# Rotation angles and their sine moved behind the merge, between two modulation rows, in a transformer kernel on one Trainium2 core

## The chip, the cores and the metric

The kernel runs on one core of a Trainium2 chip, as one launch. The metric is the device time of that launch in microseconds (us), the median of several executions. The core has a matrix engine (TensorE, PE in the profile; its weight loads are listed apart as PEld), a vector engine (VectorE, DVE), an activation engine (ScalarE, ACT) and GpSimd (POOL). SyncE (SP) issues the transfers from device memory; each engine works through its own stream of instructions in order, and the streams meet at semaphores. TensorE's clock is granted at one of two levels, 1.2 or 2.4 GHz; the profile gives the granted clock as a share of the upper one.

## The reference

One block of a first kind and two layers of a second kind, on a sequence of 256 tokens and width 1024, in float32. The part around the change is the end of the first block's mixer and its output projection:

```python
merged = jax.nn.sigmoid(p_ga) * y_a + jax.nn.sigmoid(p_gb) * y_b   # y_a = (...) @ w_a, y_b = o @ w_b
x = x + gate_m[:, None, :] * rms_norm(merged @ w_out[i], g_post_mix[i])
h = modulate(rms_norm(x, g_pre_ffn[i]), shift_f, scale_f)
```

`shift_f`, `scale_f` and `gate_f` are parts of `mod = silu(c) @ w_ada + b_ada`. The two later layers turn their queries and keys with cosines and sines of `positions * inv_freq` (`cos, sin = rope_tables(positions)`). These tables depend on the inputs alone and are used for the first time in the first of the two later mixers, hundreds of microseconds after the place where they are made.

## The kernel before

Everything lies in `build`: one function per engine, with the stages as nested functions of the same names on each engine. The order of the work on an engine is the order in which its code is written; nothing schedules it. Waits are `wait_ge` on semaphores. A `v(...)` with `v.settle()` behind it makes VectorE's next instruction wait for the end of the last.

The stages around the change, in order:

- `rwkv` ends on VectorE with the group norm (L2160 to L2164: six times three operations of 128x256). On TensorE it ends with the gate tiles 9 to 15 (L878), which ScalarE takes out of PSUM with a sigmoid (L1509).
- `angles` (VectorE, L1785 to L1805) turns the positions into angles between minus pi and pi: one conversion, one multiplication and seven operations each for `sin2` and `cos2`, all 128x256, sixteen in all; then it signals `ang_ready`. Its scratch tiles and the positions lie in `arena`, apart from all that the merge uses.
- ScalarE loads the sine's table and computes the two sines in place (L1748, L1749), and signals `trig_ready`.
- `merge` computes sixteen products of 128x256 on TensorE (L1201), into the two PSUM banks 4 and 5 in turn. Product `n` waits until VectorE has read product `n - 2` (`ym_read`). Products 0 to 7 use `w_b` and the attention's output; products 8 to 15 use `w_a`, whose two halves are the ring slots of products 8 to 11 and 12 to 15. VectorE multiplies each product by its gate (L2171 for the first eight, L2175 for the rest) and GpSimd adds each of the last eight into `merged` (L2539).
- After each of the last eight products VectorE also computes one modulation row (`ada_late`, L1809: a dot product of a 128x1024 tile with the activated condition). Rows 27 to 31 follow the merge. The rows' weights come in four tiles; SyncE loads row `r` when row `r - 4` is done.
- The modulation of the FFN is made of rows 8 to 31 (L2375 to L2378), and signals `mod_ready`, for which TensorE waits in `hand_over` behind the projection.
- `project` (TensorE, L945) multiplies `merged` by `w_out` into banks 0 to 3, one after another. ScalarE, ahead of taking the squares of each bank (`rms_of_output`, L1518 to L1529), copies the first half of the FFN's first weights (`high_up`, L1422), and VectorE makes their remainder (`low_up`, L1841).

SyncE's queue (L647 for the ring of two weight slots, L697 for the modulation rows) issues in this order: `w_b` (freed by a gate tile), the first half of `w_a` (freed by the last gate tile), the second half of `w_a` (freed by product 7), rows 22 to 25, `w_out` (freed by product 11), rows 26 to 31, the first FFN weights (freed by product 15).

Of the kernel before, what the change touches and what calls it, by code (L numbers as in the profile page):

```python
# [246 lines left out]
G_FFN1 = G_GATES + 8  # L247
# [21 lines left out]
def wait(engine, sem, value):  # L269

    if isinstance(value, int) and value <= 0:
        return
    engine.wait_ge(sem, value)


def build(nc, T, out):
    with ExitStack() as ctx:
# [3 lines left out]
        def sem(name):  # L281
            return ctx.enter_context(nc.semaphore(name))
# [49 lines left out]
        def K(name, a=0, b=None):  # L332
            if name in EARLY_AT:
                at, w = EARLY_AT[name]
                return early[:, at + a:at + (w if b is None else b)]
            at, w = CONST_AT[name]
            return const[:, at + a:at + (w if b is None else b)]
# [139 lines left out]
        ym_full = sem("ym_full")  # L477
# [87 lines left out]
        def full_count(g, more=0):  # L565

            return 16 * (g // 2 + 1) + 8 * more
# [36 lines left out]
        def since(base, k):  # L604

            return base + max(k, 0)
# [803 lines left out]
        def _(act):  # L1410
# [6 lines left out]
            def high_up(f, g, c, h, i=0):  # L1417

                if h == 0:
                    act.wait_ge(slot_full[(g + c) % 2], full_count(g + c, i))  # L1420
                wait(act, half_done, 2 * FC * f + 2 * (c - 1) + h + 1 + 2 * i if c else 0)
                F(up_hi[:, h], ring[:, (g + c) % 2, h * 2048:(h + 1) * 2048], ACT.Copy).then_inc(up_high, 1)  # L1422
# [67 lines left out]
            def high_piece(j):  # L1490

                c, n = (j // 4, j % 4) if j < 36 else (9, j - 36)
                if n == 0 or j == 2:
                    act.wait_ge(slot_full[(G_MIX1 + c) % 2], full_count(G_MIX1 + c))
                if j > 34:
                    act.wait_ge(piece_used, j - 34)
                elif j > 4:
                    act.wait_ge(cm_full, j - 2)
                f(piece[j % 3][0], ring[:, (G_MIX1 + c) % 2, n * D:(n + 1) * D], ACT.Copy).then_inc(w_high, 1)

            def channel_major(table, base, qbase, part=range(64)):
                for j, (kind, q, _, dest) in enumerate(table):
                    if j not in part:
                        continue
                    act.wait_ge(cm_full, base + j + 1)
                    if q is not None:
                        wait(act, cm_out, since(qbase, q - 2))
                        dest = raw[:, q % 3, 1:S + 1]
                    f(dest, bank[4 + j % 2][:, 0:S], ACT.Sigmoid if kind == "sigmoid" else ACT.Copy).then_inc(cm_evac, 1)  # L1509
                    if table is T1 and j == KK_ROOT:  # L1510
                        act.wait_ge(kn_clamped, 1)
                        f(norm_kk, norm_kk, ACT.Sqrt).then_inc(kn_sqrt, 1)
                    if table is T1:
                        high_piece(j + 3)
# [229 lines left out]
            act.wait_ge(s_c, 48)  # L1744
            f(c_late, c_late, ACT.Silu).then_inc(c_ready, 1)
            channel_major(TG, CM_G, 0, range(9, 16))
            act.wait_ge(ang_ready, 1)
            f(sin2[:], sin2[:], ACT.Sin)  # L1748
            f(cos2[:], cos2[:], ACT.Sin).then_inc(trig_ready, 1)  # L1749
            act.wait_ge(ym_full, 16)  # L1750
            high_up(0, G_FFN1, 0, 0)
            rms_of_output(0, DONE_MIX1)
            norm(1, 1, 2, split_of=(0, G_FFN1))
            ffn_split(0, G_FFN1, G_LAYER)
# [17 lines left out]
        def _(dve):  # L1772
# [4 lines left out]
            def angles():  # L1777

                turn_hi = 6.28125
                turn_lo = 2 * math.pi - turn_hi  # L1780
                magic = 1.5 * 2.0 ** 23
                dve.wait_ge(s_lora, 32)
                dve.wait_ge(cm_evac, CM_G + 9)
                m = turns
                v(dve.tensor_copy(posf, pos_i))  # L1785
                v.settle()
                v(ts(ang, posf, K("inv_freq2"), None, ALU.mult))
                v.settle()
                for dst, quarter in ((sin2, 0.0), (cos2, 0.25)):
                    v(ts(m, ang, 1 / (2 * math.pi), quarter, ALU.mult, ALU.add))  # L1790
                    v.settle()
                    v(ts(m, m, magic, None, ALU.add))
                    v.settle()
                    v(ts(m, m, magic, None, ALU.subtract))
                    v.settle()
                    v(stt(posf, m, -turn_hi, ang, ALU.mult, ALU.add))
                    v.settle()
                    v(stt(posf, m, -turn_lo, posf, ALU.mult, ALU.add))
                    v.settle()
                    v(ts(posf, posf, quarter * 2 * math.pi, None, ALU.add))  # L1800
                    v.settle()
                    last = ts(dst[:], posf, math.pi, -math.pi, ALU.min, ALU.max)
                    v(last)
                    v.settle()
                dve.nop().then_inc(ang_ready, 1)  # L1805

            def dot(weights, c_of, out):

                return dve.tensor_tensor_reduce(out=weights, in0=weights, in1=c_of, scale=1.0, scalar=0.0, op0=ALU.mult, op1=ALU.add, accum_out=out)  # L1809
# [14 lines left out]
            def ada_late(r):  # L1824

                dve.wait_ge(apart_full[r % 4], 16 * (r // 4 + 1))
                dot(late_tile[r % 4], c_late, mod_raw[:, 0, 4 * FIRST + r:4 * FIRST + r + 1]).then_inc(apart_used, 1)
# [338 lines left out]
            def merge():  # L2166
                dve.wait_ge(cm_evac, CM_G + 16)
                for n in range(16):
                    dve.wait_ge(ym_full, n + 1)
                    if n < 8:  # L2170
                        tt(merged[:, n * S:(n + 1) * S], bank[4 + n % 2][:, 0:S], sig[:, (8 + n) * S:(9 + n) * S], ALU.mult).then_inc(ym_read, 1)  # L2171
                    else:
                        j = n - 8
                        wait(dve, ym_ready, j - 1)
                        tt(ytmp[:, n % 2], bank[4 + n % 2][:, 0:S], sig[:, j * S:(j + 1) * S], ALU.mult).then_inc(ym_read, 1)  # L2175
                        ada_late(19 + j)
# [190 lines left out]
            v(tt(mod_gate[:, 0], mod3[:, 0, 2], PR("g_post", 0, KD), ALU.mult))  # L2367
            attention1()
            rwkv()
            angles()  # L2370
            merge()
            for r in range(27, 32):
                ada_late(r)
            dve.wait_ge(apart_used, 4 * 8)
            v(tt(mod[:, 24:48], mod_raw[:, 0, 24:48], PR("b_ada1", 24, 48), ALU.add))  # L2375
# [203 lines left out]
```

## Time and profile before

| | us |
|---|---|
| median of 3 executions | 1742.59 |
| lowest, highest | 1742.31, 1746.23 |
| the profiled execution, its own time | 1739.06 |
| its span | 1737.3 |

The profile is one execution. Its page gives each engine's busy time as a share of the span, the granted clock, and the chain that ended last. Behind the page stand views of the trace: a timeline of instructions with the idle time before each and what ended it, a table by stretches of time, and the instructions of one line. All times are counted from the start of the span. The merge lies at about 366 to 403 us, the projection at 403 to 433.

### The profile page before, as it was taken

Reading aid. Unit: us, or ns where it says so; the run is one execution under the profiler, and the core shown is the slowest. Engines: PE = TensorE matmul, PEld = TensorE weight load, DVE = VectorE, ACT = ScalarE, POOL = GpSimd, SP = SyncE. Lnnn points to the kernel's source line nnn. Section 1 sums busy time; section 2 is a strip of 40 time slices with the busy share of each in tenths; the row PEclk is TensorE's granted clock in tenths of the full one; section 3 lists DMA queues with packets and bytes.
Section 4 is the critical chain, followed back from the end, with each engine's and each line's share of the span. In section 5 each row is a group of like instructions: output and inputs, shape, how many; then the busy total and the mean of one; then the engine's idle time right before and its main releaser. Section 6 shows DMA issues by size and latency. Waiting matters only on the chain.

```text
span 1737.3 us, 31528 instructions
## 1 busy us (share of the span) xinstructions
PE 1624.2 (93%) x12924; PEld 1438.9 (83%) x12924; DVE 1136.1 (65%) x1839; ACT 700.2 (40%) x1042; POOL 210.4 (12%) x273
## 2 busy tenths in 40 slices
PE   2998988889999989999998999999999999999998
PEld 2997777774899989999895599998999898579997
DVE  6796446374787877877565378778777665465454
ACT  2443433411533354333455443335333444543333
POOL 0342344222000000000115000000000002300000
PEclk9999999999999999999999999999999999999999
DMA  9754110256587837876440477774787542144531
GB/s 392 292 214 158 49 50 3 71 206 232 216 310 299 335 128 290 327 296 265 178 189 1 151 290 291 314 290 170 310 332 289 229 187 84 55 181 183 217 148 45
DMA packets 49638, 359.05 MB, mean 207 GB/s; under 512 B 5504, under 2 KB 6144, under 8 KB 29440
## 3 DMA queue, kind: packets, MB, share of 16 engines
q1 hardware_dynamic: 49536, 357.61, 53.5%
q8 instruction: 74, 1.21, 0.3%
q14 instruction: 28, 0.23, 0.0%
HBM read 356.54 MB, written 1.05 MB: 206 GB/s over the span
## 4 chain that ended last, share of the span: by engine, by line
PE 82%; DVE 8%; issue 4%; ACT 3%; DMA 1%; POOL 1%; SPq 0%; POOLq 0%; DVEq 0%; ACTq 0%
PE psum L840 11%; PE psum L842 11%; PE psum L841 11%; PE psum L853 5%; PE psum L854 5%; PE psum L855 5%; PE psum L945 5%; PE psum L878 3%; PE psum L810 2%; PE psum L1201 2%; DMA arena<-in_ada_head 1%; PE psum L1221 1%; PE psum L1222 1%; PE psum L1223 1%; PE psum L909 1%
## 5 line engine op out<-in xcount | busy, mean ns | idle before, releaser
L840 PE MATMUL psum<-split 128*128 128x256 f32 x1600 | 453.0, 283 | 2.8 <-DVE split L1841 2.8
L842 PE MATMUL psum<-split 128*128 128x256 f32 x1600 | 452.8, 283 | 0.0
L841 PE MATMUL psum<-split 128*128 128x256 f32 x1600 | 452.8, 283 | 0.0
L840 PEld LDWEIGHTS psum<-split 128*128 128x128 f32 x1600 | 307.0, 192 | 5.5 <-DVE split L1841 3.8
L1422 ACT ACTIVATE split<-ring 128x2048 fp32r<-128x2048 f32 x110 | 210.6, 1915 | 244.8 <-PE psum L842 169.2
L841 PEld LDWEIGHTS psum<-split 128*128 128x128 f32 x1600 | 307.0, 192 | 1.8
L842 PEld LDWEIGHTS psum<-split 128*128 128x128 f32 x1600 | 307.0, 192 | 0.0
L1841 DVE TENSOR_TENSOR split<-ring,split 128x2048 fp32r<-128x2048 f32 x110 | 251.8, 2289 | 76.4 <-ACT split L1422 73.2
L1861 DVE TENSOR_TENSOR split<-ring_down,split 128x2048 fp32r<-128x2048 f32 x55 | 126.0, 2292 | 116.9 <-ACT split L1430 116.9
L853 PE MATMUL psum<-split 128*128 128x512 f32 x440 | 171.8, 390 | 0.0
L854 PE MATMUL psum<-split 128*128 128x512 f32 x440 | 171.8, 390 | 0.0
L855 PE MATMUL psum<-split 128*128 128x512 f32 x440 | 171.2, 389 | 0.0
L1809 DVE CUSTOM_DVE_ANT_0 arena<-arena,c_row 128x1024 f32<-128x1024 f32 x144 | 167.6, 1220 | 0.0
L1430 ACT ACTIVATE split<-ring_down 128x2048 fp32r<-128x2048 f32 x55 | 105.3, 1915 | 136.5 <-PE psum L855 136.5
L2437 POOL TENSOR_TENSOR x_res<-x_res,scratch 128x512 f32<-128x512 f32 x16 | 20.4, 1274 | 1049.9 <-DVE scratch L1925 822.4
L1442 ACT ACTIVATE scratch<-psum 128x512 f32<-128x512 f32 x55 | 32.9, 599 | 213.1 <-PE psum L842 210.4
L855 PEld LDWEIGHTS psum<-split 128*128 128x128 f32 x440 | 82.6, 188 | 17.6
L853 PEld LDWEIGHTS psum<-split 128*128 128x128 f32 x440 | 82.8, 188 | 15.8
L854 PEld LDWEIGHTS psum<-split 128*128 128x128 f32 x440 | 82.8, 188 | 15.3
L878 PE MATMUL psum<-hT,ring 128*128 128x256 f32 x384 | 86.7, 384 | 3.0 <-ACT hT L1475 2.9
L878 PEld LDWEIGHTS psum<-hT,ring 128*128 128x128 f32 x384 | 73.2, 192 | 14.7 <-ACT hT L1475 3.2
L1850 DVE TENSOR_TENSOR scratch<-scratch,psum 128x512 f32<-128x512 f32 x55 | 37.8, 688 | 70.7 <-ACT scratch L1442 70.7
(422 smaller groups left out, 2897.6 us busy)
## 6 DMA issues: line engine op xcount, KB each, us to landing
ring<-in_up SPq DMA_DIRECT2D x55, 2048.0 KB, 10.4
arena<-in_ada SPq DMA_DIRECT2D x168, 512.0 KB, 6.4
ring_down<-in_down SPq DMA_DIRECT2D x55, 1024.0 KB, 4.9
ring<-in_in SPq DMA_DIRECT2D x19, 2048.0 KB, 7.9
ring<-in_gates SPq DMA_DIRECT2D x4, 2048.0 KB, 8.3
arena<-in_ada_head SPq DMA_DIRECT2D x4, 1536.0 KB, 16.8
ring_down<-in_w_out SPq DMA_DIRECT2D x3, 2048.0 KB, 12.0
ring<-in_w_out SPq DMA_DIRECT2D x3, 2048.0 KB, 8.7
```

What stands on the lines that cost most here:

```text
L840: mm(dst, up_hi[:, h, a], h_hi[:, kt_], start=(kt_ == 0 and j % 2 == 0), stop=False, skip_group_check=True)
L841: mm(dst, up_hi[:, h, a], h_lo[:, kt_], start=False, stop=False, skip_group_check=True)
L842: last = mm(dst, up_lo[:, h, a], h_hi[:, kt_], start=False, stop=(kt_ == KD - 1), skip_group_check=True)
L853: mm(bank[2 * t + h], act_hi[:, c % 2, a], d_hi[:, w], start=(c == 0 and k == 0), stop=False, skip_group_check=True)
L854: mm(bank[2 * t + h], act_hi[:, c % 2, a], d_lo[:, w], start=False, stop=False, skip_group_check=True)
L855: last = mm(bank[2 * t + h], act_lo[:, c % 2, a], d_hi[:, w], start=False, stop=(c == FC - 1 and k == 1), skip_group_check=True)
L878: last = mm(bank[4 + j % 2][:, 0:S] if dst is None else dst, w[:, k * 512 + n * P:k * 512 + n * P + P], hT[:, k, :], start=(k == 0), stop= ...
L1422: F(up_hi[:, h], ring[:, (g + c) % 2, h * 2048:(h + 1) * 2048], ACT.Copy).then_inc(up_high, 1)
L1430: F(up_hi[:, 1] if c == FC - 1 else dn_hi, ring_down[:, c % 2], ACT.Copy).then_inc(dn_high, 1)
L1809: return dve.tensor_tensor_reduce(out=weights, in0=weights, in1=c_of, scale=1.0, scalar=0.0, op0=ALU.mult, op1=ALU.add, accum_out=out)
L1841: tt(up_lo[:, h], ring[:, (g + c) % 2, h * 2048:(h + 1) * 2048], up_hi[:, h].bitcast(F32), ALU.subtract).then_inc(up_low, 1)
L1861: tt(d_lo, ring_down[:, c % 2], d_hi.bitcast(F32), ALU.subtract).then_inc(dn_low, 1)
```

## The change

On VectorE, `angles()` is called after `merge()` and after modulation rows 27 to 29, ahead of rows 30 and 31, where it was called ahead of `merge()`. On ScalarE, the wait for `ang_ready` and the two sines stand behind the wait for the last product and the copy of the FFN's first weights, where they stood ahead of them. No operation is added, taken away or resized.

```diff
             channel_major(TG, CM_G, 0, range(9, 16))
+            act.wait_ge(ym_full, 16)
+            high_up(0, G_FFN1, 0, 0)
             act.wait_ge(ang_ready, 1)
             f(sin2[:], sin2[:], ACT.Sin)
             f(cos2[:], cos2[:], ACT.Sin).then_inc(trig_ready, 1)
-            act.wait_ge(ym_full, 16)
-            high_up(0, G_FFN1, 0, 0)
             rms_of_output(0, DONE_MIX1)
...
             rwkv()
+            merge()
+            for r in range(27, 30):
+                ada_late(r)
             angles()
-            merge()
-            for r in range(27, 32):
+            for r in range(30, 32):
                 ada_late(r)
```

VectorE at the start of the merge, before: the last of the group norm (L2164), the angles, then the gate products.

```order
L1792 TENSOR_SCALAR arena<-arena 128x256
L1794 TENSOR_SCALAR arena<-arena 128x256
L1796 SCALAR_TENSOR_TENSOR arena<-arena 128x256
L1798 SCALAR_TENSOR_TENSOR arena<-arena 128x256
L1800 TENSOR_SCALAR arena<-arena 128x256
L1802 TENSOR_SCALAR cos<-arena 128x256
L2171 TENSOR_TENSOR arena<-psum,arena 128x256 x8
L2175 TENSOR_TENSOR arena<-psum,arena 128x256
```

The same place in the changed kernel:

```order
L2160 TENSOR_SCALAR arena<-arena,params 128x256
L2162 TENSOR_TENSOR arena<-arena 128x256
L2164 TENSOR_TENSOR arena<-arena 128x256
L2171 TENSOR_TENSOR arena<-psum,arena 128x256 x8
L2175 TENSOR_TENSOR arena<-psum,arena 128x256
L1809 ISA xn,mod_raw<-xn,arena 128x1024
```

The gate products now follow the group norm at once; all sixteen angle operations are gone from here.

VectorE behind the merge in the changed kernel, from the last merge product (L2175) and its row 26 through rows 27 to 29 (L1809, each with a second entry for its sum) into the angles:

```order
L2175 TENSOR_TENSOR arena<-psum,arena 128x256
L1809 ISA xn,mod_raw<-xn,arena 128x1024
L1809 ISA mod_raw 128x1
L1809 ISA xn,mod_raw<-xn,arena 128x1024
L1809 ISA mod_raw 128x1
L1809 ISA arena,mod_raw<-arena 128x1024
L1809 ISA mod_raw 128x1
L1809 ISA arena,mod_raw<-arena 128x1024
L1809 ISA mod_raw 128x1
L1785 CAST arena<-arena 128x256
L1787 TENSOR_SCALAR arena<-arena,const 128x256
L1790 TENSOR_SCALAR arena<-arena 128x256
```

Before, two more L1809 (rows 30 and 31) stood where the angles now begin; they now follow the last L1802.

ScalarE between the last gate tile (L1509) and the projection's squares, the difference of the two kernels (the sines' lines have moved by two):

```order
 L1509 ACTIVATE arena<-psum 128x256 x7
-L1748 ACT_TABLE_LOAD
-L1748 ACTIVATE sin<-sin 128x256
-L1749 ACTIVATE cos<-cos 128x256
-L1422 ACTIVATE split<-ring 128x2048
+L1422 ACTIVATE split<-ring 128x2048
+L1750 ACT_TABLE_LOAD
+L1750 ACTIVATE sin<-sin 128x256
+L1751 ACTIVATE cos<-cos 128x256
 L1518 ACT_TABLE_LOAD
 L1518 ACTIVATE stat<-const 128x1
```

The table load and the sines have changed places with the copy of the FFN weights; the number of table loads is the same. TensorE's and SyncE's streams are unchanged.

## Rows read from the trace of the kernel before

**Rows 1.** The page: its first line, engines with busy time and share, the chain
```profile
span 1737.3 us, 31528 instructions
...
PE 1624.2 (93%) x12924; PEld 1438.9 (83%) x12924; DVE 1136.1 (65%) x1839; ACT 700.2 (40%) x1042; POOL 210.4 (12%) x273
...
PE 82%; DVE 8%; issue 4%; ACT 3%; DMA 1%; POOL 1%; SPq 0%; POOLq 0%; DVEq 0%; ACTq 0%
```

**Rows 2.** Timeline, TensorE, 360 to 384: start, length, instruction, count [idle before <-releaser]
```profile
366.32 1.97 PE L1201 MATMUL psum<-arena,ring 128*128 128x256 f32 x8 [0.56 <-ACT arena L1509]
373.04 11.23 PE L1201 MATMUL psum<-arena,ring 128*128 128x256 f32 x43 [4.75 <-DVE arena L2171]
```

**Rows 3.** Timeline, VectorE, the angles and the gate products of the merge
```profile
366.56 0.28 DVE L1785 CAST arena<-arena 128x256 f32<-128x256 int32 x1
...
372.06 0.29 DVE L1802 TENSOR_SCALAR cos<-arena 128x256 f32<-128x256 f32 x1
372.56 0.76 DVE L2171 TENSOR_TENSOR arena<-psum,arena 128x256 f32<-128x256 f32 x2 [0.21 <-DVE cos L1802]
...
380.21 0.42 DVE L2171 TENSOR_TENSOR arena<-psum,arena 128x256 f32<-128x256 f32 x1 [0.44 <-PE psum L1201]
```

**Rows 4.** Table by stretches: PE, PEld, DVE, ACT, POOL busy, clock, DMA, GB/s
```profile
366.30:368.30 2.00, 1.97 (x8) 1.43 (x8) 1.83 (x7) 1.18 (x1) 0.00 (x0) 1.00 0.77 221
...
373.00:380.20 7.20, 7.16 (x25) 5.96 (x26) 2.44 (x6) 0.16 (x1) 0.00 (x0) 0.76 0.00 0
380.20:401.00 20.80, 20.69 (x96) 17.86 (x94) 11.45 (x23) 0.00 (x0) 11.46 (x7) 1.00 0.90 337
...
403.10:432.60 29.50, 29.43 (x64) 12.67 (x64) 11.01 (x20) 5.66 (x11) 1.27 (x1) 0.94 0.52 184
```

**Rows 5.** Timeline, TensorE, three other pauses
```profile
146.81 0.50 PE L928 MATMUL psum<-split 128*128 128x512 f32 x1 [1.68 <-DVE split L1968]
...
240.23 0.45 PE L1071 MATMUL psum<-arena 64*64 64x64 f32 x8 [2.55 <-POOL arena L2488]
...
403.12 8.40 PE L945 MATMUL psum<-ring,arena 128*128 128x512 f32 x15 [2.23 <-POOL arena L2539]
```

**Rows 6.** Table by stretches, behind the first two of these pauses
```profile
146.80:151.80 5.00, 4.99 (x22) 4.15 (x23) 4.93 (x9) 1.06 (x1) 0.46 (x1) 1.00 0.01 2
240.20:244.00 3.80, 3.77 (x76) 3.77 (x77) 0.00 (x0) 0.98 (x2) 3.40 (x5) 0.55 0.02 4
```

**Rows 7.** The two transfers of `w_a`: issue (first and last start) and landing
```profile
L647 SPq DMA_DIRECT2D ring<-in_w_a x2: 328/328/328, 365.8 to 380.2; - x2
...
DMA to landing us min/median/max: 6.6/6.7/6.7
```

**Rows 8.** Timeline, VectorE, end of row 29, rows 30 and 31, modulation, residual half
```profile
406.37 0.08 DVE L1809 DVE_READ_ACCUMULATOR2_ANT mod_raw<- 128x1 f32 x1
407.15 1.23 DVE L1809 CUSTOM_DVE_ANT_0 xn<-xn,arena 128x1024 f32<-128x1024 f32 x1 [0.71 <-DMA xn<-in_ada]
...
409.61 1.23 DVE L1809 CUSTOM_DVE_ANT_0 xn<-xn,arena 128x1024 f32<-128x1024 f32 x1 [1.22 <-DMA xn<-in_ada]
...
411.18 0.16 DVE L2378 TENSOR_TENSOR mod_gate<-mod,params 128x8 f32<-128x8 f32 x1
...
422.30 0.69 DVE L1931 TENSOR_TENSOR x_res<-x_res,scratch 128x512 f32<-128x512 f32 x1 [0.79 <-POOL x_res L2437]
```

**Rows 9.** Timeline, ScalarE, from the sine's table to the square of bank 2
```profile
366.20 1.28 ACT L1748 ACT_TABLE_LOAD   x1
372.44 0.42 ACT L1748 ACTIVATE sin<-sin 128x256 f32<-128x256 f32 x1 [4.96 <-DVEq L1805]
372.76 0.40 ACT L1749 ACTIVATE cos<-cos 128x256 f32<-128x256 f32 x1
414.57 1.91 ACT L1422 ACTIVATE split<-ring 128x2048 fp32r<-128x2048 f32 x1 [41.41 <-DMA ring<-in_up]
...
425.72 0.60 ACT L1526 ACTIVATE arena<-psum 128x512 f32<-128x512 f32 x1 [5.85 <-PE psum L945]
```

## The prediction

> **What bounds the kernel now.** I read the page first: TensorE is busy for 93% of the 1737.3 us span, and 82% of the chain that ended last is its work [rows 1]. So a microsecond counts only where TensorE stands still or runs at its lower clock. Then I looked along TensorE's own timeline at the merge, the place of the change. It computes sixteen products, eight with the small weights (`w_b`, 4 matmul rows each) and eight with `w_a` (12 rows each). It issues 8 rows from 366.32, that is products 0 and 1, and then pauses for 4.75 us, until 373.04, with a VectorE instruction of L2171 as the releaser [rows 2]. VectorE's timeline tells why: the sixteen angle instructions begin at 366.56, the last begins at 372.06 and lasts 0.29, and only at 372.56 does the first L2171 free a PSUM bank for product 2 [rows 3]. Both banks are full and nothing else is left for TensorE to do. ScalarE and the DMA queues are not in this wait; the order of VectorE's stream makes all of it.
>
> The table by stretches shows a second part. From 373.0 to 380.2 the granted clock averages 0.76, against 1.00 before and after [rows 4]. So the pause is followed by a stretch at the lower of the two levels, 1.2 instead of 2.4 GHz, and this too belongs to its price.
>
> **What moving the angles gives.** At the full clock, 96 matmul rows take 20.8 us [rows 4], so 0.2167 us each. Eight rows from 366.32 would let the ninth be issued at 366.32 + 8 x 0.2167 = 368.05; it is issued at 373.04, hence 4.99 us. (The 4.75 of the wait is counted from the modelled end of the eighth.) The remaining 24 rows of products 2 to 7 should take 24 x 0.2167 = 5.20 us. The lower clock loses 7.2 x (1 - 0.76) = 1.73 us on them. Sum 4.99 + 1.73 = 6.72 us. A second way to it: undisturbed, product 7 is complete at 366.32 + 32 x 0.2167 = 373.25 plus 0.2 for the last matmul's end and the signal, so at 373.5; VectorE took it at 380.21 [rows 3]. The difference is again 6.7.
>
> **What is late next.** Products 8 to 11 need the first half of `w_a`. Its transfer is issued at 365.8, triggered by the last gate tile and not by the merge, and lands 6.7 us later, at 372.5 [rows 7]. TensorE would want it at 373.25: hidden by 0.75 us. This is the smallest cover in the whole change. If it were used up, each microsecond of lateness would cost one. The second half is issued when product 7 is done and moves with it; it has four products, 48 x 0.2167 = 10.4 us, for a landing of 6.6 to 6.7 [rows 7]. The later modulation rows, `w_out` and the first FFN weights are all released by merge steps and move along. VectorE's multiply (0.4 us per product) and its wait for the gate tiles keep up with a product every 0.87 us. I therefore put no new wait ahead of product 8, and pass on the full 6.7 us.
>
> **What is added behind the merge, VectorE.** In the new order the angles stand between modulation rows 29 and 30. With everything 6.7 us earlier, row 29 ends at 406.45 - 6.7 = 399.75. The angles cost the 6.0 us from 366.56 to 372.56 [rows 3] and end at 405.75. Before, rows 30 and 31 waited 0.71 and 1.22 us for their transfers [rows 8]; their issue depends on rows 26 and 27, ahead of the angles, so they have landed by 409.6 - 6.7 = 402.9 and these two gaps vanish. Two rows at 1.25 each and 0.6 of modulation arithmetic end at 408.9. The next VectorE work is the first split of FFN weights, which waits for ScalarE's copy; that copy ends at 414.57 + 1.91 - 6.7 = 409.8 [rows 9]. So the added 6.0 us fit, with 0.9 us to spare there, and with about 17 us to spare until TensorE wants the modulation at the projection's end (432.6 - 6.7 = 425.9 [rows 4]). Cost on the path: 0.
>
> **What is added, ScalarE.** The two sines and the load of their table used to stand in idle time ahead of the merge. Now they follow the weight copy: 1.28 for the table and 0.72 from the start of the first sine to the end of the second [rows 9], 2.0 us. The number of table loads stays the same, since the table of the square root was loaded after the sine's anyway. The angles are ready at 405.75, ahead of 409.8, so ScalarE doesn't wait for them. Everything up to the first residual half moves from an end at 422.99 [rows 8] to 422.99 - 6.7 + 2.0 = 418.3. The next event is projection bank 2, at 425.72 - 6.7 = 419.0 [rows 9]. So this too is hidden, by 0.7 us for that event and by 7 us before the real end of the stage, bank 3. With these covers gone the price would be 2.0 us. The Trainium skill ("ScalarE: Activation LUTs", section "What ACT_TABLE_LOAD costs") puts a switch of tables at 1.28 us and a drain of 1.38 more. By that the added piece would be 3.4 us and would pass bank 2 by 0.7, and still not bank 3; the trace agrees with the 1.28 and shows no drain, so I leave it out.
>
> **Does the lower clock go away too?** The trace has pauses of several lengths. After 1.68 us (146.81) the clock stays at 1.00; after 2.55 us (240.23) it averages 0.55 over the next 3.8 us [rows 5, 6]. After the 2.23 us at 403.12, where TensorE waits for GpSimd's last merged sum, it is 0.94 over 29.5 us [rows 4, 5], a loss of 1.8 us. A merge without its pause has only the 0.56 us before product 0, so I expect 1.00 throughout. The pause at 403 stays, moved to 396.4. The Trainium skill ("TensorE: Matmul & The Clock Gate", section "What's actually happening") says that the clock is released by activity and that how many matmuls run at the lower level varies from run to run; by that the pause at 396 could keep the full clock in some runs, and one of the shorter pauses could lose it, each by about the 1.8 us of the row. That speaks against trusting the second digit of the sum, and makes the next two cases.
>
> **The rivals.**
> A, forecast: pause and low clock both go, nothing else is late. 6.7 us. On the profiled execution 1739.06 - 6.7 = 1732.4 us (span 1730.6). The median of the runs shown is 3.5 us above that execution; from it, 1742.59 - 6.7 = 1735.9 us.
> B, the clock takes part of it back: the pause is gone, but a dip appears at another pause, or the merge still has one. 5.0 us, 1737.6. For it: runs of one kernel spread from 1742.31 to 1746.23, twice such a dip. Against it: no pause up to 1.68 us is followed by a dip.
> C, a wait on `w_a` takes the place of the wait on VectorE. If this 1.5 MB transfer took a quarter longer, 8.4 us, product 8 would start 0.9 us late: 5.8 us left, 1736.8. To lose the pause's whole value it would have to land 7.5 us late. Against it: both `w_a` transfers took 6.6 to 6.7, and no other load shares the engines at that time.
> D, a dip fewer: the pause before the projection keeps its clock. 6.7 + 1.8 = 8.5 us, 1734.1.
> E, slower: the angles' new place lands on the path. Row 29 ends at 399.75, and behind it stand 6.0 us of angles and 3.1 us of rows and arithmetic, all of which TensorE's hand-over at 425.9 waits for. From the point where row 29 ends after 425.9 - 9.1 = 416.8, some 17 us late for want of its transfer, the whole 6.0 us of angles lie behind the projection, with the 2.0 us of sines on ScalarE, and the pause there, long enough for a dip, adds 1.8 more: 9.8 against 6.7, 3.1 us slower, 1745.7. Against it: the last rows wait at most 1.22 us for a transfer now [rows 8].
> F, the change doesn't free TensorE, since something else would hold the first L2171: nothing in the trace does; its products were complete at 368.3. No change, 1742.6.
>
> **How the numbers follow.** Chances: A 0.68, B 0.12, C 0.06, D 0.09, E 0.02, F 0.03. The likeliest gives 1735.9 us, 0.38% below the median. The range 1732.0 to 1740.0 takes in A, B, C and D with a spread of about 2 us on either side, as the runs shown have, and leaves out E, F and the tails. What can be told from no change is 0.3%, 5.2 us, and A exceeds that by only 1.5 us. So I count a fifth of A, and nearly all of B and a third of C, as within 0.3%: faster 0.54 + 0.01 + 0.04 + 0.09 = 0.68, rounded to 0.69. Slower by over 0.3% would need more than E: 0.01. Within: 0.30.
>
> **What would show it.** In the changed kernel's trace the L1201 row on TensorE should run through without a pause of microseconds, with the granted clock at 1.00 up to product 15; the last merge product and the projection should stand 6.7 us earlier (projection from 396.4). VectorE's L1785 to L1802 should follow the fourth L1809 after the last L2175 and end by 406; L1809 after them should show no DMA wait. ScalarE should show copy, table load, two sines, table load in a row from about 408. A TensorE wait released by the `w_a` transfer at 373 would show C; a clock below 1.00 before 394, or a new dip later, B; a TensorE wait for `mod_ready` work after 426, E. The forecast is wrong if the merge is shorter by clearly less than 6 us, or if the stages behind it give time back.

## The result and the profile after

| | before | changed |
|---|---|---|
| median of 5 executions each, same chip | 1742.31 us | 1732.30 us |
| lowest, highest | 1739.65, 1746.23 | 1728.91, 1734.24 |
| the profiled execution, its span | 1739.06, 1737.3 | 1734.24, 1732.4 |

The ratio is 0.9949, with a 95% interval of 0.9930 to 0.9967. So the change makes the kernel faster, by 0.5% with an interval of 0.3 to 0.7%. (A ratio in this document is not that of the two medians, which here is 0.9943; the two differ by up to 0.0013.) Of all later executions one of the kernel before took 5620 us and one of the changed kernel 2326 us, and ratios and means leave these two out. The 10.0 us between the medians above are more than the 6.7 of the prediction; the profiled executions differ by 4.8. Both distances have to be explained.

TensorE's timeline of the changed kernel, over the merge and the start of the projection (start, length, instruction, count, idle time before and what ended it):

```profile
359.71 8.58 PE L878 MATMUL psum<-hT,ring 128*128 128x256 f32 x39
368.85 27.86 PE L1201 MATMUL psum<-arena,ring 128*128 128x256 f32 x128 [0.57 <-ACT arena L1509]
398.95 7.54 PE L945 MATMUL psum<-ring,arena 128*128 128x512 f32 x13 [2.23 <-POOL arena L2541]
```

The 128 rows of the merge stand in one piece; the second line of [rows 2] with its 4.75 us is gone. VectorE's timeline of the same kernel, the first and the last product of the first eight:

```profile
370.06 0.42 DVE L2171 TENSOR_TENSOR arena<-psum,arena 128x256 f32<-128x256 f32 x1 [0.90 <-PE psum L1201]
...
376.04 0.42 DVE L2171 TENSOR_TENSOR arena<-psum,arena 128x256 f32<-128x256 f32 x1 [0.44 <-PE psum L1201]
```

From TensorE's first row of the merge to the reading of product 7 it was 380.21 - 366.32 = 13.89 us [rows 2, 3], and it is 376.04 - 368.85 = 7.19 now: 6.70 less. From the first row of the merge to the first of the projection it was 403.12 - 366.32 = 36.80 [rows 2, 5], and it is 398.95 - 368.85 = 30.10: again 6.70. Behind that nothing is gained: from the first row of the projection to TensorE's first transpose of the hand-over it is 33.50 us in both profiles (403.12 to 436.62, and 398.95 to 432.45). The table by stretches (the columns of [rows 4]) has the clock at 1.00 through the merge, and still below it in the projection:

```profile
368.85:376.00 7.15, 7.15 (x33) 6.16 (x34) 3.29 (x8) 0.00 (x0) 0.00 (x0) 1.00 0.60 221
376.00:396.70 20.70, 20.70 (x96) 17.89 (x95) 11.38 (x22) 0.00 (x0) 11.45 (x7) 1.00 0.91 327
...
398.90:428.40 29.50, 29.43 (x64) 12.67 (x64) 16.25 (x36) 7.54 (x13) 1.27 (x1) 0.94 0.50 185
```

The merge itself starts 2.53 us later than in the profile of before. This is ahead of everything that was changed. Two earlier stretches, first of before, then of the changed kernel:

```profile
167.00:178.00 11.00, 8.69 (x28) 6.96 (x29) 4.33 (x29) 4.53 (x9) 3.43 (x2) 0.69 0.00 1
239.00:250.00 11.00, 8.59 (x224) 8.38 (x224) 5.12 (x14) 3.64 (x7) 7.50 (x11) 0.84 0.09 36
```

```profile
167.00:178.00 11.00, 9.38 (x25) 7.35 (x26) 3.74 (x27) 3.83 (x9) 3.43 (x2) 0.53 0.00 0
239.00:250.00 11.00, 9.13 (x176) 9.09 (x176) 2.41 (x11) 2.90 (x5) 6.46 (x10) 0.53 0.15 62
```

The instructions there are the same; the granted clock was at its lower level for longer in this one execution. So the profiled pair differs by 4.9 us of span: 2.5 lost ahead of the merge, 6.7 gained in the stage, 0.7 gained somewhere behind the hand-over. Ahead of the merge single executions differ by more than the change is worth: in the thirteen profiles of this document its first row lies anywhere from 365.18 to 373.61 us, while the time from the hand-over to the end is always 1298.4 to 1301.2. A single pair of profiles of this kernel shows what a stage gained, and not what the whole gained.

VectorE behind the merge, in the changed kernel:

```profile
402.20 0.28 DVE L1785 CAST arena<-arena 128x256 f32<-128x256 int32 x1
...
408.17 1.23 DVE L1809 CUSTOM_DVE_ANT_0 xn<-xn,arena 128x1024 f32<-128x1024 f32 x1 [0.18 <-DVE cos L1802]
409.32 0.08 DVE L1809 DVE_READ_ACCUMULATOR2_ANT mod_raw<- 128x1 f32 x1
...
410.89 0.16 DVE L2380 TENSOR_TENSOR mod_gate<-mod,params 128x8 f32<-128x8 f32 x1
412.00 2.29 DVE L1841 TENSOR_TENSOR split<-ring,split 128x2048 fp32r<-128x2048 f32 x1 [0.95 <-ACT split L1422]
...
419.43 0.69 DVE L1931 TENSOR_TENSOR x_res<-x_res,scratch 128x512 f32<-128x512 f32 x1 [0.79 <-POOL x_res L2439]
```

The angles last from 402.20 to 408.17, 6.0 us. The two waits for transfers of [rows 8] are gone, and VectorE is free 0.95 us before ScalarE's copy of the weights is done. ScalarE:

```profile
410.05 1.91 ACT L1422 ACTIVATE split<-ring 128x2048 fp32r<-128x2048 f32 x1 [41.34 <-DMA ring<-in_up]
411.98 1.28 ACT L1750 ACT_TABLE_LOAD   x1
413.27 0.42 ACT L1750 ACTIVATE sin<-sin 128x256 f32<-128x256 f32 x1
413.60 0.40 ACT L1751 ACTIVATE cos<-cos 128x256 f32<-128x256 f32 x1
414.01 1.28 ACT L1518 ACT_TABLE_LOAD   x1
...
421.55 0.60 ACT L1526 ACTIVATE arena<-psum 128x512 f32<-128x512 f32 x1 [4.55 <-PE psum L945]
```

It still waits 4.55 us for the projection's bank 2, where it waited 5.85 [rows 9].

### The profile page after: what moved, and what is told of

Same layout as the page of the kernel before. It is cut to its first block, busy times and chain, and to the rows that moved or that the text cites. A ratio compares the mean times of both kernels' runs of the same rounds, so it can differ in the third digit from the quotient of the medians.

```text
span 1732.4 us, 31528 instructions
## 1 busy us (share of the span) xinstructions
PE 1625.1 (94%) x12924; PEld 1440.6 (83%) x12924; DVE 1135.3 (66%) x1839; ACT 700.1 (40%) x1042; POOL 211.0 (12%) x273
## 4 chain that ended last, share of the span: by engine, by line
PE 83%; DVE 7%; ACT 3%; issue 3%; DMA 1%; POOL 1%; SPq 0%; POOLq 0%; DVEq 0%; ACTq 0%
PE psum L840 11%; PE psum L842 11%; PE psum L841 11%; PE psum L854 5%; PE psum L853 5%; PE psum L855 5%; PE psum L945 5%; PE psum L878 5%; PE psum L810 2%; PE psum L1201 2%; DMA arena<-in_ada_head 1%; PE psum L1221 1%; PE psum L1222 1%; PE psum L1223 1%; PE psum L909 1%
## 5 line engine op out<-in xcount | busy, mean ns | idle before, releaser
L1809 DVE CUSTOM_DVE_ANT_0 arena<-arena,c_row 128x1024 f32<-128x1024 f32 x144 | 167.7, 1222 | 0.0
L855 PEld LDWEIGHTS psum<-split 128*128 128x128 f32 x440 | 82.6, 188 | 17.5
```

Of the source, the lines that this page charges most:

```text
L855: last = mm(bank[2 * t + h], act_lo[:, c % 2, a], d_hi[:, w], start=False, stop=(c == FC - 1 and k == 1), skip_group_check=True)
```

## The experiments

The theory (M): the change is worth what the stage shows, 5.0 us of pause and 1.7 us of lower clock; all else in the first result is the draw of the clock, that is, how long the clock happens to be low in one execution and behind which pauses. The rival (N): the change really gives 10 us, and something behind the merge gains too. Smaller rivals concern the clock's part, the covers, and whose move carries the gain. A cover is the time by which something can come later before TensorE waits for it. The runs fall into four jobs, each with its own runs of the kernel before. The first gave the result above. The second has the repetition of both kernels, the clock's part and the next pause; the third has half the pause, VectorE's move alone and the two covers; the fourth has the rest.

**The same two kernels again.** First the changed one, unedited, in another job:

> The changed kernel once more. Theory M (the stage is worth 6.7 us: 5.0 us of pause and 1.7 us of lower clock; the rest of the first result is a draw of clock dips elsewhere): median 6.7 us below the kernel before, within about 2 us; from the first L1201 row to the reading of product 7 in 7.2 us, against 13.9 before. Rival N (the change gives 10 us, something behind the merge gains too): again 9 to 11 us.

Median 1734.25 us (12 executions) against 1740.11 (31): 5.9 us, ratio 0.9971 (0.9953 to 0.9989). Merge, projection and hand-over on TensorE:

```profile
365.41 27.86 PE L1201 MATMUL psum<-arena,ring 128*128 128x256 f32 x128 [0.57 <-ACT arena L1509]
394.59 7.13 PE L945 MATMUL psum<-ring,arena 128*128 128x512 f32 x16 [1.32 <-POOL arena L2541]
...
426.39 1.73 PE L772 MATMUL psum<-const,xn 128*128 128x128 f32 x8 [4.07 <-DVE xn L1891]
```

Product 7 is read at 372.59, 7.18 us after the first row, and the stage (first row of the merge to first row of the projection) takes 29.18 us.

> The kernel before against itself, with nothing changed: how far two medians of one kernel lie apart. Theory M needs 1 to 3 us between medians, in steps of about 1.7 us of lost clock in single executions; rival N needs well under 1 us. Merge as before: 13.9 us from the first L1201 row to the reading of product 7.

Median 1741.09 us (12) against 1740.11 (31) for the very same kernel, ratio 1.000 (0.9984 to 1.0016). So a median of a dozen executions moves by a microsecond with nothing changed. Single executions of the kernel before reached from 1733.41 to 1745.51. The same stretch in this profile:

```profile
373.61 1.97 PE L1201 MATMUL psum<-arena,ring 128*128 128x256 f32 x8 [0.56 <-ACT arena L1509]
380.31 27.85 PE L1201 MATMUL psum<-arena,ring 128*128 128x256 f32 x120 [4.74 <-DVE arena L2171]
409.48 7.13 PE L945 MATMUL psum<-ring,arena 128*128 128x512 f32 x16 [1.32 <-POOL arena L2539]
...
441.29 1.06 PE L772 MATMUL psum<-const,xn 128*128 128x128 f32 x8 [4.07 <-DVE xn L1891]
```

Product 7 is read at 387.49, after 13.88 us, and from 380.3 to 387.5 the clock averages 0.76, as in the first profile. The stage takes 409.48 - 373.61 = 35.87 us against 29.18: 6.69 less in the changed kernel, in a second, separate pair. From the projection to the hand-over it is 31.81 and 31.80 us. So nothing behind the merge gains, which is what N needed.

> The changed kernel a third time, since single executions of one kernel spread over 10 us and medians over 2. Theory M: median 5.5 to 8 us below the kernel before; after the time that the granted clock lost is taken off each execution (span times one minus the mean clock), 5.0 us below, the pause alone. Rival N (10 us, some of it behind the merge): 9 us or more, and more than 6 with the lost clock taken off.

Median 1734.37 (12) against 1740.22 (29): 5.85 us, ratio 0.9962 (0.9945 to 0.9979). Without the two executions named with the result, which fell into this job, the medians are 1733.93 and 1740.18, 6.2 us apart. The results give each execution's span and mean granted clock, and so what the clock lost (span times one minus the mean):

| | mean time | lost to the clock | the rest |
|---|---|---|---|
| before, second job (31) | 1739.61 | 23.28 | 1716.33 |
| changed, second job (12) | 1733.02 | 21.94 | 1711.08 |
| before, fourth job (28) | 1740.04 | 22.98 | 1717.06 |
| changed, fourth job (11) | 1732.86 | 21.26 | 1711.60 |
| before against itself, second job (12) | 1741.06 | 25.66 | 1715.40 |

By the means the change gives 6.6 and 7.2 us. The rest differs by 5.25 and 5.46 us and the clock's part by 1.34 and 1.72. These lie near the 5.0 of the pause and the 1.7 of the dip, but the split is rough, for two reasons. The kernel before has 0.9 us less in the rest when it is compared with itself. And the last column takes the lost clock off as if each microsecond of it cost one, which the single executions do not bear out. Over the 191 of them in these three jobs, each compared with the mean of its own kernel and job, the time rises by 0.59 us for each microsecond lost to the clock; this accounts for 90% of the spread (as variance), and 1.0 us (standard deviation) is left. Taken off at that rate, the change gives 5.8 and 6.2 us, each give or take 0.7, where M gives 5.0 + (1 - 0.59) x 1.7 = 5.7. N wanted 9 or more in medians and more than 6 in the rest; both medians and both rests fall short, and 10 us, a ratio of 0.9943, lies outside both intervals. The first job's 10.0 us came from five executions a side, with the kernel before at 1742.3 where 31 and 29 executions gave 1740.1 and 1740.2, and the changed one at 1732.3 where 12 gave 1734.3 and 1734.4. The clocks of those five executions of the kernel before are not on record, so that they drew a lower clock is likely and not shown.

**The clock's part alone.** The kernel before, and TensorE computes something in the pause:

```diff
+                    if n == 2:
+                        for _ in range(10):
+                            mm(bank[6][:, 0:S], ident, o1[:, 0:S], start=True, stop=True)
                     wait(pe, ym_read, n - 1)
```

> The kernel before, with the angles ahead of the merge, but TensorE computes ten unused 128x256 products (20 rows, 4.3 us) into a free PSUM bank while it would wait for product 2. Their results are not used. Theory M: the wait for VectorE ends as before, but the clock stays at 1.00, so product 7 is read 1.7 us earlier than before (12.2 us from the first L1201 row of product 0 instead of 13.9); time 1.7 us below before. Rival (the clock part of the sum was not due to the pause): clock falls all the same, no change. Rival (the stretch is slow for another reason, such as PSUM or VectorE): clock 1.00 and still 7.2 us for products 2 to 7.

TensorE's timeline in it, then its table by stretches:

```profile
371.70 1.97 PE L1204 MATMUL psum<-arena,ring 128*128 128x256 f32 x8 [0.57 <-ACT arena L1512]
373.50 4.48 PE L1197 MATMUL psum<-arena,const 128*128 128x256 f32 x20
```

```profile
373.60:378.30 4.70, 4.38 (x21) 3.52 (x19) 4.13 (x13) 0.50 (x2) 0.00 (x0) 1.00 0.62 258
378.40:384.10 5.70, 5.70 (x26) 4.97 (x27) 2.62 (x7) 0.13 (x1) 0.00 (x0) 1.00 0.00 0
```

The wait for VectorE ends as before, but the clock stays at 1.00 and product 7 is read 12.18 us after the first row (product 8 at 386.47, less the 2.59 of one product, less 371.70). Before it was 13.89: 1.7 us less, with the pause intact. The stage is 405.88 - 371.70 = 34.18 us, against 35.87 of the kernel before in the same job: again 1.69 less. This is the clock's term by itself. In the medians it is lost among the draws, 1738.44 against 1740.11 us, ratio 0.9991 (0.9971 to 1.0011).

**Half the pause.** The conversion, the multiplication and the sine's seven operations stay ahead of the merge, the cosine's seven stand behind row 29; ScalarE is as in the changed kernel. Against the kernel before, on VectorE (the argument says which half `angles` computes):

```diff
-            angles()
+            angles((0,))
             merge()
-            for r in range(27, 32):
+            for r in range(27, 30):
+                ada_late(r)
+            angles((1,))
+            for r in range(30, 32):
                 ada_late(r)
```

> The sine's half of the angles (nine operations, about 3.2 us) stays ahead of the merge, the cosine's half stands between rows 29 and 30; ScalarE as in the changed kernel. The pause ahead of product 2 should be 2.4 us by issue instead of 5.0. Theory M: 2.4 us of the gain are gone, and 1.7 more if the clock falls after it, as after the other pauses of 2.2 us and more: product 7 is read 9.6 or 11.3 us after the first L1201 row. If the lower clock needed a pause as long as the one of 4.75 us, 9.6.

```profile
372.20 26.17 PE L1201 MATMUL psum<-arena,ring 128*128 128x256 f32 x120 [2.00 <-DVE arena L2173]
```

The pause is 2.00 us and the 120 rows take 26.17 us, at a clock of 1.00; in the kernel before they took 27.85 (403.12, less the wait of 2.23, less 373.04 [rows 2, 5]). So the shorter pause has cost no clock in this execution. Product 7 is read at 377.68, 9.45 us after the first row (9.6 was expected for a pause without a lower clock, 11.3 for one with it). The stage is 399.69 - 368.23 = 31.46 us, 2.27 more than the 29.19 of VectorE's move alone, which ran in the same job. Median 1736.03 against 1739.80 us, ratio 0.9991 (0.9976 to 1.0006), which can't tell it from either. It gives no safe length of a pause: the same pauses elsewhere in the kernel are followed by a lower clock in some profiles and not in others (last section).

**VectorE's move alone.** As the changed kernel, with ScalarE's stream of the kernel before. Against the changed kernel:

```diff
-            act.wait_ge(ym_full, 16)
-            high_up(0, G_FFN1, 0, 0)
             act.wait_ge(ang_ready, 1)
             f(sin2[:], sin2[:], ACT.Sin)
             f(cos2[:], cos2[:], ACT.Sin).then_inc(trig_ready, 1)
+            act.wait_ge(ym_full, 16)
+            high_up(0, G_FFN1, 0, 0)
```

> The angles moved as in the changed kernel, but ScalarE's stream as before: its sines stand ahead of the wait for the last product and of the copy of the FFN weights. Theory M: only VectorE's move carries the gain; ScalarE then waits for the angles until about 408 and copies the weights after them, at or shortly after the time that their transfer lands. Same time as the changed kernel, within 0.3 us in the stage. Rival: ScalarE's part carries some of it, 1 to 2 us slower.

The stage takes 397.69 - 368.50 = 29.19 us, as with ScalarE's part (29.18 in the second job, with the same wait of 1.32 us ahead of the projection). The median is 1733.39 against 1739.80 us, 6.4 less, ratio 0.9965 (0.9949 to 0.9981). ScalarE waited for the angles, did its sines from 408.27 and then waited 1.35 us more for the weights:

```profile
408.27 0.42 ACT L1748 ACTIVATE sin<-sin 128x256 f32<-128x256 f32 x1 [38.61 <-DVEq L1805]
408.59 0.40 ACT L1749 ACTIVATE cos<-cos 128x256 f32<-128x256 f32 x1
410.34 1.91 ACT L1422 ACTIVATE split<-ring 128x2048 fp32r<-128x2048 f32 x1 [1.35 <-DMA ring<-in_up]
```

All of the stage's gain is VectorE's. ScalarE's part is neither needed nor harmful there.

**The cover of `w_a`.** Case C, brought about by a later issue of the first half:

```diff
+            sp.wait_ge(ym_full, 4)
             for c in range(2):
                 load(g + 5 + c, T["w_a"][c], (ym_full, 8 + 4 * (c + 1)))
```

> The changed kernel, with the first half of w_a issued only after product 3 of the merge, about 3.6 us later than now. Case C of the prediction, made on purpose: it lands 2.9 us after product 8 wants it, by the cover of 0.75 us that the sum found; TensorE waits 2.9 us there and loses 1.7 more to the clock, 4.6 us above the changed kernel. If the cover were larger than that (3 us or more), no change.

```profile
376.91 22.67 PE L1202 MATMUL psum<-arena,ring 128*128 128x256 f32 x96 [3.04 <-DMA ring<-in_w_a]
```

TensorE waits 3.04 us for the transfer, and the next 5.1 us run at a mean clock of 0.67, 1.7 us lost:

```profile
376.90:382.00 5.10, 5.09 (x16) 4.20 (x17) 0.51 (x2) 0.00 (x0) 0.01 (x1) 0.67 0.79 327
```

The stage is 400.90 - 366.72 = 34.18 us, 5.0 more than the 29.19 of VectorE's move alone in the same job; the expectation was 4.6. The transfer was issued at 370.4, 3.7 us after the first row of the merge, where the changed kernel has it 0.55 ahead (368.3 and 368.85): 4.2 us later and not 3.6. Product 8 started at 376.91 and not at 366.72 + 6.93 = 373.65, so 3.3 us late, which leaves a cover of about 1.0 us. So the cover was nearly as small as the sum said, and C was a real danger that did not come about: in the changed kernel the transfers took 6.3 to 6.6 us. Median 1735.10 us, ratio to the kernel before 0.9986 (0.9968 to 1.0005). It is 1.7 above VectorE's move alone, and 2.8 in the means, where the stage of one profile lost 5.0. The draws are of that size; whether the wait is as long in every execution is not shown.

**The cover behind the merge.** The angles four times over in their new place, the signal to ScalarE after the last:

```diff
-            angles()
+            for again in range(4):
+                angles(again == 3)
```

> The changed kernel with the angles computed four times over in their new place (three times for nothing, with the same result), so 17.5 us more on VectorE and the sines as much later. It measures the cover behind the merge. By the sum, the hand-over of the modulation (about 410.9 in the changed kernel) has 17 us until the projection's end at 428.4 and the first residual half (end 420.1) some 8: I expect the first half of the residual to come 5 to 9 us too late and TensorE's first row of the hand-over as much later. If the cover were as small as the 0.9 us that low_up has, the loss would be 16 us.

```profile
416.13 7.03 PE L945 MATMUL psum<-ring_down,arena 128*128 128x512 f32 x16
...
435.72 1.94 PE L772 MATMUL psum<-const,xn 128*128 128x128 f32 x8 [12.56 <-DVE xn L1892]
```

This variant was executed once (1737.87 us), so only its trace is read. From the first row of the projection's last bank to the hand-over's first transpose it is 19.59 us, where the changed kernel in the second job has 426.39 - 415.29 = 11.10. Of 17.5 us added (the angles last from 400.13 to 423.60, 23.5 us against 6.0), 8.5 came out behind, so 9.0 were still hidden. VectorE runs without a wait from the angles through rows 30 and 31 and the split of weights until 428.7, and the first half of the residual ends at 432.25, behind the end of the projection (423.16). So the 0.95 us ahead of the split of weights were no bound; the chain through the first half of the residual was, as expected.

**The next pause.** The merge was cured, and the projection begins with a wait of its own, 2.23 us for GpSimd's last sum. The projection's first bank needs the merged tiles one by one:

```diff
                         for k in range(KD):
+                            if staged and t == 0 and h == 0:
+                                pe.wait_ge(ym_ready, k + 1)
                             last = mm(bank[2 * t + h], lhs(k, t), w[:, k * 512:(k + 1) * 512], start=(k == 0), stop=(k == KD - 1))
...
-            pe.wait_ge(ym_ready, 8)
             pe.wait_ge(row_ready, 1)
-            project(G_GATES + 7, lambda k, t: merged[:, k * S + t * P:k * S + (t + 1) * P], 1)
+            project(G_GATES + 7, lambda k, t: merged[:, k * S + t * P:k * S + (t + 1) * P], 1, staged=True)
```

> The changed kernel, and the projection's first eight products wait each for its own merged tile instead of all for the last one. Theory M applied to the next pause: TensorE's 2.23 us wait for GpSimd's last sum goes, and with it the dip of 1.7 us behind it; 3.9 us below the changed kernel, 10.6 below the kernel before. Rival: the wait moves to the eighth product of the projection (GpSimd's sum is then long done, so I don't expect it) or the dip comes all the same: 2.2 us below the changed kernel.

The projection follows the merge with no pause, at a clock of 1.00:

```profile
373.31 27.86 PE L1203 MATMUL psum<-arena,ring 128*128 128x256 f32 x128 [0.57 <-ACT arena L1510]
401.31 7.11 PE L947 MATMUL psum<-ring,arena 128*128 128x512 f32 x16
```

```profile
401.30:428.90 27.60, 27.59 (x64) 12.06 (x64) 18.04 (x39) 7.43 (x13) 1.99 (x2) 1.00 0.62 222
```

Merge to projection is 28.00 us. Median 1730.08 us (8 executions) against 1740.11, ratio 0.9946 (0.9924 to 0.9968). And once more:

> The kernel with the projection that waits tile by tile, once more, for its median against the kernel before: theory M gives 6.7 + 1.3 to 3.9 us below it, 8 to 10.6; more if the pause before the projection is 2.23 us long with a dip in most executions, less if it is 1.32 without.

Median 1730.18 (12) against 1740.22, ratio 0.9951 (0.9934 to 0.9968). Twice 10.0 us below the kernel before, and the lowest medians here. The 4.2 us below the changed kernel are more than its traces show. Merge to projection is 28.00 and 27.89 us in the two profiles, 1.2 to 1.3 less than the 29.18 of the changed kernel where that waited 1.32 us. Only where it waits 2.23 us, with a lower clock behind, does the difference come to 3.8 (from the merge to the hand-over, 63.60 and 59.78). The means are 2.1 and 1.8 us apart. How often the longer wait occurs is not on record.

**How long is GpSimd's sum?** In the second and third job TensorE's wait before the projection was 1.32 us in all profiles of kernels that have it, also in the unchanged one, and GpSimd's last sum took 0.72 us instead of 1.64. There VectorE waited for row 26's transfer (0.59 us in the changed kernel of the second job) and began the row 0.46 us or more after the sum. The test, on the changed kernel:

```diff
+                        if j == 7:
+                            dve.wait_ge(ym_ready, 8)
                         ada_late(19 + j)
```

> The changed kernel, and VectorE starts modulation row 26 only when GpSimd's last merged sum is done. Theory S (GpSimd's 128x256 addition takes 1.64 us because L1809 runs on VectorE beside it, and 0.72 alone): the last of the eight L2541 takes 0.72 us in every execution and TensorE's wait for it is 1.32 us instead of 2.23; up to 0.9 us less, and no lower clock behind it. Rival (its length hangs on the transfers that were late in the second job, not on VectorE): 1.64 us where row 26's transfer has landed in time, and VectorE's rows 0.7 to 1.6 us later for nothing.

GpSimd's last two sums and VectorE's row behind the second:

```profile
394.54 1.63 POOL L2543 TENSOR_TENSOR arena<-arena 128x256 f32<-128x256 f32 x1 [0.95 <-DVE arena L2175]
397.13 0.72 POOL L2543 TENSOR_TENSOR arena<-arena 128x256 f32<-128x256 f32 x1 [0.96 <-DVE arena L2175]
...
397.90 1.23 DVE L1809 CUSTOM_DVE_ANT_0 xn<-xn,arena 128x1024 f32<-128x1024 f32 x1 [0.85 <-POOL arena L2543]
```

Here it was the added wait that kept VectorE away, and the sum took 0.72; the changed kernel in the same job, where the row had landed, had 1.64 and a wait of 2.23. So the length hangs on L1809 running beside it. The median is 1731.47 us, 2.9 below the changed kernel in that job (1.0 in the means); the two intervals overlap (0.9941 to 0.9975 and 0.9945 to 0.9979), so only the row and the wait are shown.

## Why the prediction was right

- **The bound.** TensorE's stillness and its clock were the right things to read. Removing 4.99 us of pause and 1.73 of lower clock was put at 6.72. One pair of profiles gave 6.70, both to product 7 and to the projection; a second pair gave 6.70 and 6.69.
- **The clock.** That it belongs to the price of a pause was argued from rows before; the busy pause shows it apart, at 1.7 us. What the prediction took from these rows, that a pause's length tells whether the clock falls, is not borne out: after the same pause of 2.55 us (its row at 240.23) the clock stayed at 1.00 in three of the thirteen profiles.
- **What is late next.** `w_a` was not late. Its cover in the changed profile: issued at 368.3, landed by 374.9, wanted at 368.85 + 6.93 = 375.8, so 0.9 us against the 0.75 of the sum, and about 1.0 in the run that used it up.
- **VectorE's added 6.0 us.** All hidden, with 0.95 us to spare ahead of the split of weights (0.9 forecast). The 17 us until the hand-over of the modulation was not the cover that counted: the residual's first half ends the slack earlier, at 9.0 us. Case E was therefore priced from the wrong point; the deadline of row 29 is nearer than 416.8. It did not matter for the result. That lateness there does reach TensorE is shown: 17.5 us more of VectorE's work behind row 29 came out as 8.5 at the hand-over.
- **ScalarE's added 2.0 us.** Table load and sines take 2.02 us. The first residual half ends 1.43 us before bank 2 (420.12 and 421.55), where the sum said 0.7; part of the 2.0 had been a wait for bank 1 before (0.28 us ahead of the square at 418.85), and the weights landed 0.3 us sooner after their issue (9.6 us against 9.9). This cover is no fixed number: in the second job's profile of the changed kernel the first half ends at 417.87, 2.4 us after the square of bank 2 began, and the hand-over is still not later. So bank 2 was not the event that counted.
- **The size.** The forecast was 6.7 us and 1735.9 us; the first comparison gave 10.0 and 1732.3, inside the range of 1732.0 to 1740.0 by 0.3 us, which is luck. The mechanism was not short by 3.3 us; the two repetitions give 5.9 in the medians and 6.6 and 7.2 in the means. The step that was too weak is the starting point, the median of three executions: it was 2.4 to 2.5 us above what 31 and 29 executions gave, and the 3.5 us between it and the profiled execution were carried along as if they were fixed. Single executions of one kernel spread over 10 us or more, 90% of the variance goes with the granted clock, and three or five executions don't average it out.
- **The rivals.** B and D, a dip more or less, are no separate cases: every execution draws its own set. D's pause has an outcome of its own besides: it was 1.32 us long with the clock at 1.00 in eight profiles and 2.23 us with a lower clock in three, by whether VectorE's row 26 runs beside GpSimd's sum. C and E stayed away, and were shown to be real when provoked (C fully, E with the point moved). F is refuted.

## What to carry to other kernels

Work with no deadline, such as a table for a later stage, should not stand in an engine's stream ahead of the operation that frees another engine's buffers: its cost here was its length plus what the waiting engine's clock lost after it. Before moving it, look for the first transfer that the freed stage will want; here its cover was about 1 us. And when a stage is shown to be cured, compare stage with stage in the traces, since single executions of one kernel differed here by more than the change gave.

## What the hardware showed beyond that

- The clock's draw. One and the same unchanged stretch (167 to 178 us) lost 11 x 0.31 = 3.4 us to the clock in the profile before and 11 x 0.47 = 5.2 after. Single executions had a mean granted clock from 0.981 to 0.993, which is 33 to 12 us lost in 1740. A microsecond lost this way cost 0.59 us of time, over the 191 executions of the three later jobs. In the first pair of profiles the two stretches shown above lost 5.2 us more and the merge started 2.5 us later, which agrees with that; why it is less than one no run here shows.
- The same pause with and without a lower clock behind it. In the 4 us after the 2.55 us pause at about 240 us the clock averaged 0.50 to 0.68 in ten profiles and 1.00 in three. After a pause of 4.6 to 5.0 us at about 37 us it was 0.50 in five and 1.00 in eight. After one of 2.23 us at about 915 us it was below 1.00 in twelve, and 1.00 in one. A pause of 1.25 us at about 286 us was followed by a clock of about 0.6 in five of the thirteen. So the trace of one execution tells what a pause cost in it, and not what it costs.
- GpSimd's 128x256 addition takes 0.72 us alone and 1.64 beside VectorE's L1809, while L1809 takes 1.22 us beside it and 1.23 alone. Where the sum began first, by 0.46 us or more, it kept its 0.72. In the changed kernel the row that starts first (397.10, VectorE) keeps its length and the sum (from 397.26) ends 0.6 us after it; the next row on VectorE, begun during the sum, takes 1.74. It looks as if the two took turns. The Trainium skill ("GPSIMD Engine Reference", section "Specifications") says that GpSimd's SBUF interfaces are shared with VectorE and contend with VectorE instructions that have two SBUF inputs, as L1809 does; the trace agrees, with 0.9 us for this shape.
